# A cumulation in two rounded parts, and attention scores taken out of their banks before their maxima

## The reference, cut to what matters

```python
# stick breaking: z = q k / 8, per head and query t over keys s < t
u = jnp.where(mask, jax.nn.log_sigmoid(-z), 0.0)        # = -softplus(z)
between = lax.cumsum(u, axis=3, reverse=True) - u       # sum over the keys between s and t
a = jnp.where(mask, jnp.exp(jax.nn.log_sigmoid(z) + between), 0.0)
out_b = a @ v
# top-k attention: logits = q k / 8 + bias, masked outside the top 64 keys
p = jax.nn.softmax(logits, axis=-1);  out_a = p @ v
```

## Time and profile before

| | |
|---|---|
| median of 3 runs | 1094.49 us (1094.03 to 1096.38) |
| profiled execution | 1094.11 us |
| its span | 1092.4 us |
| busy share of the span | PE 97%, PEld 85%, DVE 78%, ACT 50%, POOL 5% |
| granted TensorE clock, mean | 0.999 of full |

### The profile page before, as it was taken

The page is one execution under the profiler, slowest core; times in us unless marked ns, Lnnn a source line. Parts: engine busy times, 40 slices in busy tenths (PEclk is TensorE's granted clock), DMA queues, the critical chain, the costliest instruction groups (busy, mean ns, idle before and its releaser), DMA issues.

```text
span 1092.4 us, 16231 instructions
## 1 busy us (share of the span) xinstructions
PE 1062.3 (97%) x6159; PEld 927.3 (85%) x6159; DVE 854.6 (78%) x931; ACT 548.9 (50%) x664; POOL 50.3 (5%) x78
## 2 busy tenths in 40 slices
PE   3999999999999999999999999999999999999997
PEld 2999999889988788888978888898887778888886
DVE  6899888678887788887778988877876787666665
ACT  4444343564765654444564444454654456444452
POOL 1000000011121100000010000000100000000001
PEclk9999999999999999999999999999999999999999
DMA  9999997546424599997569999844562536767651
GB/s 342 381 400 391 388 394 261 178 118 221 148 78 154 178 337 312 325 316 234 203 232 343 344 367 342 281 167 135 179 209 100 192 117 212 234 216 233 218 176 58
DMA packets 147141, 265.26 MB, mean 243 GB/s; under 512 B 9770, under 2 KB 104471, under 8 KB 141975
## 3 DMA queue, kind: packets, MB, share of 16 engines
q1 hardware_dynamic: 145376, 261.30, 69.4%
q0 software_dynamic: 1056, 3.17, 0.8%
q10 hardware_dynamic: 662, 0.16, 0.1%
HBM read 263.34 MB, written 1.27 MB: 242 GB/s over the span
## 4 chain that ended last, share of the span: by engine, by line
PE 87%; DVE 4%; DMA 3%; ACT 2%; issue 2%; SPq 1%; POOL 1%; POOLq 0%; DVEq 0%; ACTq 0%
PE ps L1957 18%; PE ps L1888 12%; PE ps L1889 11%; PE ps L1890 11%; PE ps L1963 9%; PE ps L1938 6%; PE ps L1941 6%; PE ps L1940 6%; DMA w_raw<-in_w_ffn_up 1%; ACT w_hi L824 1%; DMA arena<-in_w_ada 1%; DVE w_lo L1209 1%; DVE y_row L1370 1%; PE ps L1908 1%; PE ps L2432 1%
## 5 line engine op out<-in xcount | busy, mean ns | idle before, releaser
L1209 DVE TENSOR_TENSOR w_lo<-w_raw,w_hi 128x2048 fp32r<-128x2048 f32 (+2 forms) x169 | 380.7, 2255 | 104.8 <-ACT w_hi L824 103.8
L824 ACT ACTIVATE w_hi<-w_raw 128x2048 fp32r<-128x2048 f32 (+2 forms) x169 | 317.5, 1883 | 248.8 <-PE ps L1890 93.7
L1957 PE MATMUL ps<-nT_both,w_hi 128*128 128x512 f32 x864 | 210.8, 391 | 0.0
L1957 PEld LDWEIGHTS ps<-nT_both,w_hi 128*128 128x128 f32 x864 | 158.6, 188 | 31.0
L1938 PE MATMUL ps<-nT_both,w_hi 128*128 128x256 f32 x576 | 164.3, 285 | 0.0
L1940 PE MATMUL ps<-nT_both,w_hi 128*128 128x256 f32 x576 | 162.9, 283 | 0.0
L1941 PE MATMUL ps<-nT_both,w_lo 128*128 128x256 f32 x576 | 162.9, 283 | 0.0
L1291 DVE SCALAR_TENSOR_TENSOR arena<-arena,c_act 128x3072 f32<-128x3072 f32 (+2 forms) x49 | 129.4, 2650 | 0.5 <-DMA arena<-in_ada_w 0.5
L1888 PE MATMUL ps<-w_hi,hT_hi 128*128 128x512 f32 x320 | 125.0, 391 | 0.0
L1889 PE MATMUL ps<-w_lo,hT_hi 128*128 128x512 f32 x320 | 125.0, 391 | 0.0
L1890 PE MATMUL ps<-w_hi,hT_lo 128*128 128x512 f32 x320 | 124.5, 389 | 0.0
(11 more groups left out here) (296 smaller groups left out, 1217.7 us busy)
## 6 DMA issues: line engine op xcount, KB each, us to landing
arena<-in_w_ada SPq DMA_DIRECT2D x16, 1536.0 KB, 9.2
arena<-in_ada_w SPq DMA_DIRECT2D x16, 1536.0 KB, 8.5
w_raw<-in_w_in SPq DMA_DIRECT2D x44, 512.0 KB, 4.6
w_raw<-in_ffn_w_down SPq DMA_DIRECT2D x44, 512.0 KB, 4.1
w_raw<-in_w_ffn_gate SPq DMA_DIRECT2D x42, 512.0 KB, 6.7
w_raw<-in_w_ffn_up SPq DMA_DIRECT2D x42, 512.0 KB, 7.7
w_raw<-in_w_ffn_down SPq DMA_DIRECT2D x42, 512.0 KB, 4.6
w_raw<-in_ffn_w_gate SPq DMA_DIRECT2D x42, 512.0 KB, 4.1
```

What stands on the lines that cost most here:

```text
L824: copy = lambda o, i: act.activation(o, i, ACT.Copy)
L1209: dve.tensor_tensor(lo(s, n), raw(s, n), hi(s, n).bitcast(F32), ALU.subtract).then_inc(lo_ready[s], 1)
L1957: pe.matmul(ps[:, i, :], hi(s)[:, cols], nT_both[:, 4 * half + k].rearrange("p a n -> p (a n)"), start=(half == 0 and k == 0), stop=False, ...
```

## The change

- The constants `tri` and `ones` get rounded copies `tri_r` and `ones_r`, made by ScalarE. They are 0 and 1, so rounding changes nothing.
- The masked softplus is split: ScalarE copies four heads into `cut_hi` (rounded), VectorE writes the rest into `cut_lo` (over `e_sb`). TensorE multiplies both parts with the rounded constants: first the high parts of heads 0 to 3, then their low parts, then high and low for each of heads 4 to 7.
- `split_hi(0,5)` moves from ahead of exp(-|z|) to between the two halves of the ln; `split_lo(0,5)` moves to between the two max-adds. `split_hi(1,6)` and the first `cut` stand ahead of group 4's eviction, `split_hi(0,6)` behind group 5's. `split_lo(0,6)` moves behind the first four scores of `a`.
- VectorE takes the scores of four heads out of their banks one after the other, without links, then forms the maxima of the four. `lmax_ready` counts each maximum.

The diff, without declarations of tiles and semaphores:

```diff
@@ ScalarE
             split_hi(*piece1(1, 5))
+            act.wait_ge(idx_acc, 2 * H)
+            copy(ones_r[:], ones[:]).then_inc(const_ready, 1)
+            copy(tri_r[:], tri[:]).then_inc(const_ready, 1)
             for h in range(H):
                 act.wait_ge(z_mm, h + 1)
                 act.activation(e_sb[:, h, :], ps[:, 4 + h % 4, 0:CAUSAL], ACT.Abs, scale=DH ** -0.5).then_inc(z_abs, 1)
-            split_hi(*piece1(0, 5))
             act.wait_ge(z_abs, H)
             act.activation(e_sb[:], e_sb[:], ACT.Exp, scale=-1.0).then_inc(z_ln, 1)
             act.wait_ge(z_ln, 1)
             for half in range(2):
                 heads = slice(HALF * half, HALF * half + HALF)
                 act.activation(e_sb[:, heads], e_sb[:, heads], ACT.Ln, bias=1.0).then_inc(z_ln, 1)
+                if half == 0:
+                    split_hi(*piece1(0, 5))
+            def cut(half):
+                heads = slice(HALF * half, HALF * half + HALF)
+                act.wait_ge(u_masked, 2 * half + 2)
+                copy(cut_hi[:, heads], e_sb[:, heads]).then_inc(cut_hi_ready, 1)
+            split_hi(*piece1(1, 6))
+            cut(0)
             transposed_group(4, TKA)
-            split_hi(*piece1(1, 6))
+            cut(1)
+            transposed_group(5, TQA)
             split_hi(*piece1(0, 6))
-            transposed_group(5, TQA)
             split_hi(*out1[1, 0])
...
-                    act.wait_ge(lmax_ready, h + 1)
+                    act.wait_ge(lmax_ready, 2 * h + t + 1)
@@ VectorE
+            def cut_rest(half):
+                heads = slice(HALF * half, HALF * half + HALF)
+                dve.wait_ge(cut_hi_ready, half + 1)
+                dve.tensor_tensor(cut_lo[:, heads], e_sb[:, heads], cut_hi[:, heads].bitcast(F32), ALU.subtract)\
+                    .then_inc(cut_lo_ready, 1)
...
-            split_lo(*piece1(0, 5))
             dve.wait_ge(z_out, H)
             for half in range(2):
                 heads = slice(HALF * half, HALF * half + HALF)
                 dve.wait_ge(z_ln, half + 2)
                 dve.scalar_tensor_tensor(e_sb[:, heads], z_sb[:, heads], 0.0, e_sb[:, heads], ALU.max, ALU.add).then_inc(u_ready, 1)
+                if half == 0:
+                    split_lo(*piece1(0, 5))
             split_lo(*piece1(1, 6))
-            split_lo(*piece1(0, 6))
+            cut_rest(0)
+            cut_rest(1)
...
-            for h in range(H):
-                dve.wait_ge(l_mm, h + 1)
-                link(dve.scalar_tensor_tensor(u_sb[:, h, :], ps[:, 4 + h % 4, 0:CAUSAL], DH ** -0.5, u_sb[:, h, :],
-                                              ALU.mult, ALU.add))
-                dve.sem_inc(l_out, 1)
-                for t in range(T):
-                    cols = slice(0, S) if t else slice(S, CAUSAL)
-                    m = stat[:, 16 + 2 * h + t:17 + 2 * h + t]
-                    link(dve.tensor_reduce(m, u_sb[:, h, cols], AX.X, ALU.max, negate=True))
-                dve.sem_inc(lmax_ready, 1)
+            for first in (0, HALF):
+                for h in range(first, first + HALF):
+                    dve.wait_ge(l_mm, h + 1)
+                    dve.scalar_tensor_tensor(u_sb[:, h, :], ps[:, 4 + h % 4, 0:CAUSAL], DH ** -0.5, u_sb[:, h, :],
+                                             ALU.mult, ALU.add).then_inc(l_out, 1)
+                if first == 0:
+                    split_lo(*piece1(0, 6))
+                for h in range(first, first + HALF):
+                    dve.wait_ge(l_out, h + 1)
+                    for t in range(T):
+                        cols = slice(0, S) if t else slice(S, CAUSAL)
+                        m = stat[:, 16 + 2 * h + t:17 + 2 * h + t]
+                        dve.tensor_reduce(m, u_sb[:, h, cols], AX.X, ALU.max, negate=True).then_inc(lmax_ready, 1)
@@ TensorE
-            for h in range(H):
-                if h % HALF == 0:
-                    pe.wait_ge(u_masked, 2 * (h // HALF) + 2)
-                if h >= 4:
-                    pe.wait_ge(r_out, h - 3)
-                else:
-                    pe.wait_ge(z_out, h + 5)
+            def cumulated(x, h, start, stop):
                 b = ps[:, 4 + h % 4, :]
-                pe.matmul(b[:, 0:CAUSAL], tri[:], e_sb[:, h, :], start=True, stop=False, skip_group_check=True)
-                pe.matmul(b[:, P:S], ones[:], e_sb[:, h, S:CAUSAL], start=False, stop=True,
-                          skip_group_check=True).then_inc(r_mm, 1)
+                pe.matmul(b[:, 0:CAUSAL], tri_r[:], x[:, h, :], start=start, stop=False, skip_group_check=True)
+                return pe.matmul(b[:, P:S], ones_r[:], x[:, h, S:CAUSAL], start=False, stop=stop, skip_group_check=True)
+
+            pe.wait_ge(const_ready, 4)
+            pe.wait_ge(cut_hi_ready, 1)
+            for h in range(HALF):
+                pe.wait_ge(z_out, h + 5)
+                cumulated(cut_hi, h, True, False)
+            pe.wait_ge(cut_lo_ready, 1)
+            for h in range(HALF):
+                cumulated(cut_lo, h, False, True).then_inc(r_mm, 1)
+            pe.wait_ge(cut_lo_ready, 2)
+            for h in range(HALF, H):
+                pe.wait_ge(r_out, h - 3)
+                cumulated(cut_hi, h, True, False)
+                cumulated(cut_lo, h, False, True).then_inc(r_mm, 1)
```

More of the change, by code:

```diff
@@ L146, in program @@
         ob_T = qkT[:, TQI]
+        cut_hi = nc.alloc_sbuf_tensor_at("cut_hi", [P, H, CAUSAL], F32R, offset=arena_at).ap()
+        cut_lo = nc.alloc_sbuf_tensor_at("cut_lo", [P, H, CAUSAL], F32R, offset=arena_at + 4 * 13312).ap()
+        tri_r = nc.alloc_sbuf_tensor_at("tri_r", [P, P], F32R, offset=arena_at + 4 * 17152).ap()
+        ones_r = nc.alloc_sbuf_tensor_at("ones_r", [P, P], F32R, offset=arena_at + 4 * (17152 + P)).ap()
         toe_rows = carve(0, CAUSAL)
@@ L234, in program @@
         osq_done = sem("osq_done")
+        cut_hi_ready, cut_lo_ready = map(sem, ["cut_hi_ready", "cut_lo_ready"])
         pT_dve = sem("pT_dve")
```

## The result

The changed kernel takes 1096.72 us (median of 11 runs, 1096.37 to 1098.74), the kernel before 1094.17 in the same comparison (11 runs, 1093.93 to 1096.38): ratio 1.0025, 95% interval 1.0017 to 1.0032. It is slower by 2.55 us. The forecast was 1094.9, 0.39 us more than before by its sum and no difference that can be measured; the time lies at the upper edge of the range.

What follows compares the result with a forecast made beforehand. TensorE was taken as the bound, busy 8.00 of 8.00 us in the cumulation's stretch. +0.65 - 0.26 = +0.39 us on the profiled 1094.11 gave 1094.5, stated as a median of 1094.9; range 1092.7 to 1096.8.

Steps and rivals of the forecast that it cites:

- TensorE's own work: Cumulation: a head costs 0.57 us in rounded products; eight take 4.54 instead of 7.04, 2.5 less if nothing starves it.
- Rival A: Cumulation: the 128-column rounded products cost 0.22 us each, not 0.11; +1.3 in all, 1095.8 us; chance 0.23.
- ScalarE's chain: Before the cumulation: Exp starts at 288.38 instead of 290.31, its Ln result reaches VectorE at 294.06, `cut(1)` starts at 305.50.
- The starved masks: GpSimd's selects slow beside VectorE's splits (2.68 us, 0.63 alone), so masks of heads 4 to 7 end at 305.44.
- Rival B: Before head 4: selects get in early, no starving, first subtraction 2.2 us earlier; -1.8 in all, 1092.7 us; chance 0.14.
- The hole: Between heads 3 and 4 of the cumulation TensorE idles 3.1 us, until VectorE's first subtraction; it resumes at 309.37.
- Scores ahead of maxima: Second logits group: with four scores out of their banks before it starts, its wait is gone, -0.26 us.
- +0.65 at the value half: End of the first four logits heads: 313.26 instead of 312.61, 0.65 us later, with the clock at 1.00.
- rival C: The idle 3.1 us lets TensorE's clock fall, 1.6 us lost, +2.0 in all; with further delay 1096.5 to 1097.4; chance 0.10.

Runs made afterwards that it cites:

- experiment 7: The changed kernel with both splits of piece (0, 5) back at their old places, ahead of the Exp and of the sums: 1097.11 us, ratio 1.0012.
- filled kernel: The changed kernel with 13 unread products of 512 columns put where TensorE idles behind the low parts of heads 0 to 3: 1097.54 us, ratio 1.0015.
- experiment 4: The changed kernel with heads 0 to 3 subtracted before the second rest, and high parts of heads 4 to 7 before their low parts: 1096.13 us, ratio 1.0007.
- Experiments 1 and 2: The changed kernel with 13 unread products in TensorE's idle stretch, 1097.54 us; then repeated, 1097.18, beside the changed kernel again, 1097.80.
- experiment 8: The changed kernel with only VectorE's split of piece (0, 5) moved behind the second sum: 1097.31 us, ratio 1.0012.
- experiment 3: The changed kernel with 4 unread products of 512 columns behind the low parts of heads 0 to 3: 1097.04 us, ratio 1.0008.
- experiment 5: The changed kernel with only heads 0 to 3 split, heads 4 to 7 in full fp32: 1094.26 us, ratio 0.9993; repeated 1094.43, ratio 0.9988.
- experiment 9: The changed kernel with both splits of piece (0, 5) at their old places and the first four subtractions ahead of the second rest: 1096.76 us, ratio 1.001.

## Why the prediction was wrong, point by point

- **TensorE's own work: right.** Pairs go every 0.287 us (0.284 forecast), so a head costs 0.57. Rival A falls: beside the 0.174 of 384 columns the 128 add 0.113, where A had 0.22. (The starts alone would mislead: from `ones_r` to `tri_r` 0.06 us, from `tri_r` to `ones_r` up to 0.23; the pair is what is priced.)
- **ScalarE's chain: right to 0.2 us.** Exp at 288.55 (288.38 forecast), first result at VectorE 294.27 (294.06), `cut(1)` 305.63 (305.50).
- **The starved masks: right.** 305.60 against 305.44; `cut_rest(1)` from 307.15 (307.05). Rival B falls. What the prediction did not see is that the early Exp is worth less than nothing to the masks here (experiment 7): with the split between the sums they end 1.7 us later than with both splits at their old places, although the Exp starts 1.93 us earlier.
- **The hole: right.** 2.94 us (3.1 forecast), ended by the first subtraction; TensorE resumes at 309.52 (309.37).
- **Scores ahead of maxima: right in sign, 0.16 to 0.19 us for 0.26.** The pause of 0.09 ahead of the second logits group did not go.
- **+0.65 at the value half, with the clock at 1.00: this step failed.** The wait alone costs 0.73 (A to B of the filled kernel against before), close to the 0.65; 1.55 of the clock come on top, 0.21 is a later start of the stretch: 0.73 + 1.55 + 0.21 = 2.49. The sum had no term for the clock.

So the mechanism that decided was the prediction's own rival C. Its size was good (1.6 forecast, 1.55 measured; 1096.5 forecast, 1096.72 measured), its place was right (down somewhere from 309 to 315), and it got a chance of 0.10. The argument that pushed it down was that at the kernel's end the clock stood for 4.4 us after the last product. That row was misread. It shows one case of how late the clock follows a pause, and the prediction took it as leave to pause that long. In the changed kernel the clock fell at 310.3, 3.8 us after the hole had opened and when TensorE was busy again. Nor is the row a steady one: over the thirteen profiled executions the clock fell 2.0 to 5.1 us after the last product had ended (4.8 in the kernel before). The earliest is the reordered kernel of experiment 4, whose last product starts at 1085.98:

```profile
1088.00:1089.00 1.00, 0.00 (x0) 0.00 (x0) 0.62 (x2) 0.00 (x0) 0.29 (x1) 0.69 0.00 0
```

Only a pause with work behind it can tell whether the work is hit, and no such row of that length was in the argument; the other evidence, the longest hole since the opening and the first eight products at 1.2 GHz, spoke for C.

The Trainium skill ("TensorE: Matmul & The Clock Gate", Part 1: The HAM clock gate) calls the low clock the default that only activity releases. Experiments 1 and 2 agree: products that nobody reads, in the same hole, kept it at 1.00.

Why a large saving moved the time the wrong way: 2.5 us of matmul time were saved (2.35 where nothing starved it, experiment 8) in a stretch where TensorE was the bound by little. The two rests (2.18 and 1.76 us) and two cuts needed for it stand on engines that the masks pass through, and for heads 4 to 7 they fall behind the masks. What was saved became a wait, and the wait cost the clock. Splitting heads 0 to 3 alone keeps half of the saving (half of 2.5 us is 1.25; A to B shows 1.12), since their cut and rest lie beside group 5.

Open: what exactly makes the clock fall. Once the clock had first risen (at 28 to 31 us), the thirteen profiled executions have 21 waits of TensorE of more than 1.1 us before its last product. All five from 2.8 to 3.4 us were followed by a fall (2.94 twice, 2.95, 2.77 and 3.40). Of the sixteen from 1.1 to 2.3 us four were: 1.53 and 1.17, which stood 1.4 and 3.0 us behind one of 0.41, then 1.79 and 2.02; twelve were not, 2.24 and 2.03 among them. The same wait shows both. Before the z scores TensorE waited 1.79 us in experiment 3 (first two rows) and 1.78 us in the repeated run of experiment 5 (last two), and lost the clock behind the first alone:

```profile
285.74 0.94 PE L2265 MATMUL ps<-arena 64*128 64x256 f32 x3 [1.79 <-DVE arena L1611]
287.00:290.00 3.00, 3.00 (x16) 2.60 (x13) 2.41 (x6) 2.33 (x5) 0.00 (x0) 0.50 0.83 314
...
285.78 0.94 PE L2263 MATMUL ps<-arena 64*128 64x256 f32 x3 [1.78 <-DVE arena L1610]
287.00:290.00 3.00, 3.00 (x26) 2.79 (x23) 2.86 (x6) 2.97 (x6) 0.00 (x0) 1.00 0.82 307
```

So neither the longest pause nor the sum of the pauses decides alone, and one profiled execution of a kernel with pauses of this size is one sample, not the rule. Open too is where 0.4 us or so of the filled kernel's runs at 0.998 or more went (1096.26 against 1095.28 of before, 0.98, where 0.73 - 0.17 = 0.56 is explained).

## What to carry to other kernels

Before a matmul is made cheaper, follow its operands back: if making them puts new steps behind the last result on the chain, split only the part whose operands are early. Price a pause of TensorE of about three us at the pause plus some 1.6 us of clock, where TensorE is the bound behind it: five of five such pauses cost it here. One of 1.1 to 2.3 us cost it in four cases of sixteen, so take several executions. The granted clock in windows of 1 us *behind* the pause tells, while the row at the end of the kernel doesn't. An operation moved ahead on one engine gains only what its successor's engine can take: look at what VectorE runs beside GpSimd before counting an earlier start as time won.

## What the runs showed of the hardware

- Of the nine stretches at 1.2 GHz behind a pause in the thirteen executions, eight lasted 3.4 us (in this mixer, from 286.9 in experiment 3, and in the second mixer in experiments 1, 2 and 9). The one of experiment 8 lasted 6.8 us, 301.1 to 307.9.
- The fall can come after the pause: 0.8 us after TensorE had resumed in the changed kernel, 1.6 us after in experiment 9, within the pause in experiment 8 (clock 0.77 in 300 to 302, products only from 302.00).
- GpSimd's select of 128x512 took 0.61 us with VectorE idle and 2.63 beside VectorE's two-input operations on SBUF (1.22 and 5.26 for two, experiment 8), within one execution.
